# One modulation tile per projection piece instead of ten behind the first

## The reference

```
cond = silu(c)
for l in range(2):
    mod = cond @ w_ada[l] + b_ada[l]                      # 1024 x 6144 weights
    sh_m, sc_m, g_m, sh_f, sc_f, g_f = split(mod, 6)
    h = rmsnorm(x, norm_g[l, 0]) * (1 + sc_m) + sh_m
    y = mixer(h @ w_in[l], ...) @ w_out[l]                # differential attention, MLA, Mamba-2
    x = x + g_m * rmsnorm(y, norm_g[l, 1])
    h = rmsnorm(x, norm_g[l, 2]) * (1 + sc_f) + sh_f
    x = x + g_f * rmsnorm(squared_relu_mlp(h), norm_g[l, 3])
```

## Time and profile before

| | us |
|---|---|
| median of three runs | 1821.45 |
| the profiled execution | 1823.54 |
| its span in the profile | 1822.3 |
| TensorE busy | 1541.4 |
| VectorE busy | 1005.5 |
| ScalarE busy | 780.0 |
| GpSimd busy | 209.0 |

### The profile page before, as it was taken

How to read it: one execution, slowest core, us unless ns; L and a number is a source line. 1 busy time by engine, 2 the same in 40 slices (tenths; PEclk the granted TensorE clock), 3 DMA queues, 4 the chain that set the end, 5 groups by cost and what they waited for, 6 DMA issues and landing times. The chain is left out here.

```text
span 1822.3 us, 21645 instructions
## 1 busy us (share of the span) xinstructions
PE 1541.4 (85%) x8851; PEld 1287.5 (71%) x8851; DVE 1005.5 (55%) x1254; ACT 780.0 (43%) x1137; POOL 209.0 (11%) x337
## 2 busy tenths in 40 slices
PE   2588779998488879999889897878977589999996
PEld 2587669897486769998778787546856466666664
DVE  6635547666833534444563423795144566666665
ACT  3264345444263534454443222313100266666662
POOL 5021100000131000000781001220001000000000
PEclk9787889999688889999899998679978689999998
DMA  9834247776741035554433222000312359999982
GB/s 341 302 126 141 80 172 268 281 240 227 264 143 58 1 116 185 187 187 157 129 116 116 93 70 82 1 0 24 106 57 73 139 190 344 353 342 345 341 322 93
DMA packets 134585, 310.32 MB, mean 170 GB/s; under 512 B 6239, under 2 KB 99766, under 8 KB 114902
## 3 DMA queue, kind: packets, MB, share of 16 engines
q1 hardware_dynamic: 130326, 299.18, 46.4%
q0 software_dynamic: 3584, 8.71, 1.9%
q10 hardware_dynamic: 576, 1.05, 0.2%
HBM read 307.87 MB, written 1.05 MB: 170 GB/s over the span
## 5 line engine op out<-in xcount | busy, mean ns | idle before, releaser
L301 DVE TENSOR_TENSOR mlp_weights_lo<-weights,mlp_weights_hi 128x2048 fp32r<-128x2048 f32 x64 | 146.5, 2291 | 68.5 <-ACT mlp_weights_hi L291 67.6
L242 PE MATMUL bank<-mlp_in_hi,mlp_weights_hi 128*128 128x256 f32 x512 | 147.2, 288 | 10.3 <-DVE mlp_in_lo L685 10.3
L3492 DVE TENSOR_TENSOR expert_pair_lo<-weights,expert_pair_hi 128x2048 fp32r<-128x2048 f32 x53 | 119.9, 2290 | 63.9 <-ACT expert_pair_hi L3483 63.9
L243 PE MATMUL bank<-mlp_in_lo,mlp_weights_hi 128*128 128x256 f32 x512 | 146.8, 287 | 0.0
L244 PE MATMUL bank<-mlp_in_hi,mlp_weights_lo 128*128 128x256 f32 x512 | 146.7, 287 | 0.0
L291 ACT ACTIVATE mlp_weights_hi<-weights 128x2048 fp32r<-128x2048 f32 x64 | 121.9, 1908 | 56.0 <-issue 46.5
L242 PE MATMUL bank<-expert_pair_hi,x_block_hi 128*128 128x512 f32 x280 | 114.0, 407 | 5.2 <-issue 5.2
L244 PE MATMUL bank<-expert_pair_hi,x_block_lo 128*128 128x512 f32 x280 | 110.3, 394 | 0.0
L243 PE MATMUL bank<-expert_pair_lo,x_block_hi 128*128 128x512 f32 x280 | 110.2, 394 | 0.0
L242 PEld LDWEIGHTS bank<-mlp_in_hi,mlp_weights_hi 128*128 128x128 f32 x512 | 100.3, 196 | 12.1 <-issue 11.1
L553 DVE SCALAR_TENSOR_TENSOR ada<-weights,cond,ada 128x2048 f32<-128x2048 f32 x42 | 98.6, 2347 | 8.7 <-DMA weights<-in_w_ada 6.9
(11 more groups left out here) (738 smaller groups left out, 3816.4 us busy)
## 6 DMA issues: line engine op xcount, KB each, us to landing
weights<-in_w_ada SPq DMA_DIRECT2D x48, 1024.0 KB, 5.3
weights<-in_w_in SPq DMA_DIRECT2D x45, 1024.0 KB, 5.1
weights<-in_expert_w_gate SPq DMA_DIRECT2D x35, 1024.0 KB, 4.8
weights<-in_w_up SPq DMA_DIRECT2D x32, 1024.0 KB, 5.5
weights<-in_w_down SPq DMA_DIRECT2D x32, 1024.0 KB, 5.1
weights<-in_expert_w_up SPq DMA_DIRECT2D x18, 1024.0 KB, 6.2
weights<-in_expert_w_down SPq DMA_DIRECT2D x18, 1024.0 KB, 6.8
expert_raw<-in_expert_w_up SPq DMA_DIRECT2D x17, 1024.0 KB, 5.7
```

Of the source, the lines that this page charges most:

```text
L242: pe.e.matmul(out, lhsT[0], rhs[0], start=start, stop=False)
L243: pe.e.matmul(out, lhsT[0], rhs[1], start=False, stop=False)
L301: dve.e.tensor_tensor(lo, ring.view(name), hi.bitcast(F32), SUB).then_inc(*dve.mark(*self.key, "low", n))
L3492: dve.e.tensor_tensor(pair[1][:, :, part], expert_raw(s, kind, n), pair[0][:, :, part].bitcast(F32), SUB).then_inc(*dve.mark("expert", "lo ...
```

## The change

In both layers and on all three engines the middle program of the projections' weave is replaced. `in_turn(ada, 9, 1)` lets one round pass without modulation work, and then issues one step in each of the next nine rounds:

```
+def in_turn(program, count, after):
+    for _ in range(after):
+        yield STEP
+    for _ in range(count):
+        yield from some_steps(program, 1)
+        yield STEP

-yield from weave(projections_tensor(c, s, l), some_steps(ada, 10), begun_tensor(c, s, l))
+yield from weave(projections_tensor(c, s, l), in_turn(ada, 9, 1), begun_tensor(c, s, l))
```

More of the change, by code:

```diff
@@ L1772, in first_block_vector @@
         yield from modulated_cols_vector(c, dve, c.turn_banks if l else c.row_banks, s.hT, s.h_pair, s.in_scale_m, s.mod[:, 0:8], "mixer in", l)
-        yield from weave(projections_vector(c, s, l), some_steps(ada, 10), begun_vector(c, s, l))
+        yield from weave(projections_vector(c, s, l), in_turn(ada, 9, 1), begun_vector(c, s, l))
         yield from meet(c, "vector", l, "rows", "proj")
@@ L1810, in first_block_scalar @@
         yield from modulated_cols_scalar(c, act, c.turn_banks if l else c.row_banks, s.hT, s.h_pair, s.in_scale_m, s.mod[:, 0:8], "mixer in", l)
-        yield from weave(projections_scalar(c, s, l), some_steps(ada, 10), begun_scalar(c, s, l))
+        yield from weave(projections_scalar(c, s, l), in_turn(ada, 9, 1), begun_scalar(c, s, l))
         yield from meet(c, "scalar", l, "rows", "proj")
```

## The result

| | before | after |
|---|---|---|
| median (lowest to highest) | 1821.41 (1820.93 to 1822.4) | 1795.29 (1790.95 to 1796.08) |
| runs | 4 | 4 |
| profiled execution | 1823.54 | 1796.08 |
| its span | 1822.3 | 1794.8 |

The ratio is 0.9851 [0.9834, 0.9868]: 26.1 us faster by medians, 27.5 in the profiled executions. The forecast was 1789.5, so 5.8 us of the expected gain are missing. Lines from about 170 on stand 9 lines further down in the changed kernel: L500 is L509, L242 to L244 are L251 to L253, L553 is L562, L780 is L789, L1533 is L1542.

A forecast was written before the change was run, and what follows sets the result against it. TensorE, busy for 85% of the span, was taken as the bound. Layer 0's terms of -14.9 us and layer 1's of -17.0 make -31.9, taking the median of 1821.45 to 1789.5 us; range 1784 to 1796, chance 0.68.

The forecast's parts named there:

- The two stalls: TensorE's waits in the projections, 18.2 us in layer 0 and 17.5 in layer 1, go: -23.4 and -18.9 us.
- A: Projections: the pieces can't be fed at this pace, half of the rounds lose 1.5 us: 1803 us; chance 0.12.
- B: Projections: each tile's landing is waited for, a round lasts 10.7 us in place of 5.8: 1867 us; chance 0.03.
- C: No change within the measure: the stall returns at the next late thing, such as the `dt` products' loads; chance 0.03.
- the ring: Projections' tile transfers: four slots are ahead and each tile is asked for two rounds before its use.
- Round 3: Layer 0: a tile between piece 3's copy and the `dt` work delays piece 5's low part: +1.3 us.
- The latent variance: Round 6, both layers: a tile issued ahead of it delays the root that TensorE waits for: +1.6 us each.
- The end of group 1: Layer 0, moved to round 9 behind the last product: +4.1 us, and +0.5 for contention with GpSimd's rotation.
- The convolution sums: Layer 0, GpSimd: held back by up to one tile, 2.35 us each, within slack: 0, at most 1 us.
- branches: Layer 0, nine steps in place of eight: +1.0 us (-1 to +3); layer 1: 0 (-3 to +3).
- one of my own three signs of being wrong: VectorE waits for DMA in most rounds; layer 0's projections, or either layer's branches, take over 3 us more than forecast or before.
- Rival D: More gain: layer 1's branches lose a 3 us stall, layer 0's tiles hide wholly (3.5 us): 1783 us; chance 0.14.

The follow-up runs named there:

- the begun branches first: The changed kernel with the branches' first parts issued ahead of the modulation's step in each round of the projections' weave: 1782.53 us, ratio 0.9787.
- the own step: The changed kernel with the tenth modulation step moved out of the branches' weave to right behind the projections' weave: 1787.06 us, ratio 0.9806.
- ten steps: The changed kernel with the branches' first parts first and ten modulation steps in ten rounds from round 0, none left over: 1788.43 us, ratio 0.9817.
- both edits: The changed kernel with the branches' first parts first in each round and the tenth step back behind the projections: 1779.75 us, ratio 0.9757.

## Why the prediction was right, and where it was off

**The two stalls** came as forecast, -24.1 against -23.4 and -19.9 against -18.9. Pieces 1 and 2 take 5.76 us each and the `dt` products start at 62.4, so rivals A, B and C are out: the ring keeps pace with two tiles per piece. VectorE waited for weight transfers for 5.3 us between 43 and 200 us before, and the view after has no such wait. It has one of 1.9 us for which it names nothing, and ScalarE has two, 6.7 us in all as before; transfers may be behind them, but TensorE doesn't wait for them. What VectorE waits for is ScalarE's high part, 21.7 us in five waits, the slack in which the tiles hide. VectorE's timeline after, layer 0: a tile, and the low part behind it, which in round 3 is the late one.
```profile
53.55 2.29 DVE L310 TENSOR_TENSOR mixer_weights_lo<-weights,mixer_weights_hi 128x2048 fp32r<-128x2048 f32 x1 [7.93 <-ACT mixer_weights_hi L300]
...
75.56 2.34 DVE L562 SCALAR_TENSOR_TENSOR ada<-weights,cond,ada 128x2048 f32<-128x2048 f32 x1
...
79.40 2.28 DVE L310 TENSOR_TENSOR mixer_weights_lo<-weights,mixer_weights_hi 128x2048 fp32r<-128x2048 f32 x1
...
97.36 2.82 DVE L562 SCALAR_TENSOR_TENSOR ada<-weights,cond,ada 128x2048 f32<-128x2048 f32 x1
100.10 0.75 DVE L976 TENSOR_SCALAR latent_small<-latent_small 128x2 f32<-128x2 f32 x2
...
131.25 0.17 DVE L934 TENSOR_SCALAR dt_z<-dt_exp 128x16 f32<-128x16 f32 x1
...
136.27 0.15 DVE L991 TENSOR_SCALAR lam<-lam 128x1 f32<-128x1 f32 x1
```

**Round 3** cost TensorE the 1.3 us of the forecast. What the forecast left out is the clock behind such a wait: 1.9 us more in most profiles.

**The latent variance**: +1.25 and +2.4 against 1.6 twice (the wait itself grew by 2.0 in layer 0). The rows show the mechanism as told: the tile at 97.36 is ahead of the variance at 100.10. With the begun branches first the cost is 0.2.

**The end of group 1**: +4.82 against 4.1 + 0.5 (the 7.4 us that the forecast had for before are 7.27). VectorE's chain sets it, as the step said (TensorE waits 5.3 us for `lam`). The softplus chain takes 5.17 us from 131.25 to the end of `lam`, and took 4.68 before; GpSimd's rotation beside it takes 3.97 (131.27 to 135.24) after 3.86. So 0.5 us are there, on VectorE's side and not GpSimd's, where I had put them. That GpSimd's reads are what held VectorE up is likely and not shown.

**The convolution sums** were put at 0, and cost the end nothing that shows. GpSimd's timeline after:
```profile
78.59 6.43 POOL L1000 TENSOR_TENSOR conv<-conv,taps 128x256 f32<-128x256 f32 x3 [6.80 <-ACT taps L857]
85.19 2.10 POOL L1015 TENSOR_TENSOR k_rows<-lora,rope_cos 128x32 f32<-128x32 f32 x1 [0.17 <-POOL conv L1000]
87.24 2.30 POOL L1016 TENSOR_TENSOR rope_half<-lora,rope_sin 128x32 f32<-128x32 f32 x1
```
Three sums take 6.4 us, where they took 2.3 to 2.4 when nothing lay beside them, and L1015 takes 2.10 where L1006 took 0.25. VectorE beside the last two:
```profile
84.35 2.82 DVE L310 TENSOR_TENSOR mixer_weights_lo<-weights,mixer_weights_hi 128x2048 fp32r<-128x2048 f32 x1
87.09 2.34 DVE L562 SCALAR_TENSOR_TENSOR ada<-weights,cond,ada 128x2048 f32<-128x2048 f32 x1
```
L1015 ends at 87.3, where L310 ends at 87.2, and L1016 at 89.5, where L562 ends at 89.4. ScalarE starts to use the sum at 91.38, so 6 us of slack were there. The Trainium skill (SBUF — State Buffer, "Who interferes with whom") has it that the one with two SBUF inputs on VectorE and the reader on GpSimd shut each other out for a whole instruction; by that rule, the trace agrees.

**The step that failed is "branches".** I took +1.0 for layer 0 and 0 for layer 1, inside bounds of -1 to +3 and -3 to +3, from the number of steps. They measured +3.50 and +3.14, both just over the upper bound that I had set, and "over 3 us more" in the branches was one of my own three signs of being wrong. The reasoning "TensorE is busy there, the tile lies beside it" counted VectorE's time, and neither the order nor the clock. In layer 0 the later end of the group waits for a bank that the copy to `hT` has to free, in layer 1 it stands ahead of what the state-space branch waits for. The experiment with the own step returned both (-0.02 and -0.90), so it is shown that the place of the step makes the loss in this order of a round. The way from there to the time is known in part. Of the 3.5 us 1.3 are idle time, and of the 3.1 none; the rest is slower products. With the begun branches first the wait for the bank is still 3.4 us, and layer 0's branches take 0.5 us less than before. Which part of layer 0's 3.5 us is the bank, and which the tile more, was not separated.

**Not foreseen and not explained**: -3.2 in the second block, and +0.9 and +0.5 in `w_out` and the MLPs (0.0 in layer 0 of the kernels with the begun branches first, and with ten steps; again 0.9 with both edits). "Nothing behind the first block depends on when it starts" was thus wrong by 3.2 us, and the error was luck: it made the forecast look better than its terms. Without it the change is worth 24.3 us, 7.6 less than the sum said, and the median would be near 1798.5, outside the range of 1784 to 1796. Rival D's time, 1783, was within reach of the same idea, but in another order: the two edits together gave 1779.75.

## What to carry to other kernels

A long block of one engine's in-order work is best cut at the size of its neighbour's step, but each slice then costs what the slack of its round doesn't hold: put it behind the short chains of that round, not ahead. Count what the cutting leaves over, since one step moved out of the weave cost 3.5 and 3.1 us in stretches that nobody had meant to change. A wait of one to five us on TensorE should be priced with the slow clock that can follow it, and where work must go somewhere, the wait in front of a long stretch is a good place for it.

## What the runs showed of the hardware

The granted clock can fall to 0.5 or 0.57 with TensorE busy for the whole window, behind 32 products of 8 columns or a wait of 1.5 us, and in another execution of the same kernel it stays at 1.00 there. Each such fall cost 1.5 to 3.1 us, and two of them were 4.5 of the 5.1 us between two profiled executions of one kernel. The same block of code runs in 543.9 or 540.7 us, the same in all three profiles of the kernel before and in all three of the changed one, with the clock at 0.86 or 1.00 in a window of it. The first 10 us of layer 0's branches hold 51 products at a clock of 0.50 behind a wait of 5.3 us, and 71 at 0.94 where no wait is in front.
